# A four-layer hybrid trunk: another order of the attention layer's sums, and a last down projection over the 512 output positions

## The reference

```python
def mla_mixer(a, w_down, g_cq, g_ckv, w_uq, w_ukv, g_qhead, g_khead, w_o, cos, sin, cid):
    down = a @ w_down
    c_q = rms_norm(down[..., :384], g_cq);  c_kv = rms_norm(down[..., 384:640], g_ckv);  k_pe = down[..., 640:]
    q = (c_q @ w_uq).reshape(B, L, 8, 192);  kv = (c_kv @ w_ukv).reshape(B, L, 8, 256)
    k = concatenate([kv[..., :128], k_pe for every head]);  v = kv[..., 128:]
    q = rms_norm(q, g_qhead);  k = rms_norm(k, g_khead)          # then rope on the last 64
    # real queries in blocks of 128 see the keys of their own and earlier chunks of 64 and the meta tokens
    s = q k^T * 192 ** -0.5;  p = softmax(mask(s));  o = p v
    return o @ w_o

def conv_glu_ffn(a, w_up, conv_w, conv_b, w_down):
    u = causal_depthwise_conv3(a @ w_up, conv_w) + conv_b
    gate, val = split(u, 2)
    return (silu(gate) * val) @ w_down

def reference(...):
    h = concatenate([meta_tokens (16), x (512)])                 # 528 positions, D = 1024
    for layer in range(4):
        h = h + mixer[layer](rms_norm(h));  h = h + conv_glu_ffn(rms_norm(h))
    return h[:, 16:]
```

## Time and profile before

| what | value |
|---|---|
| median of three runs | 3211.4 us (3210.82 to 3211.84) |
| profiled execution | 3212.88 us |
| its span, first to last instruction | 3211.1 us |
| mean granted TensorE clock | 0.948 of 2.4 GHz |
| attention layer, about | 30 to 400 us |
| last down projection, about | 3078 to 3211 us |

### The profile page before, as it was taken

The page is one execution under the profiler, slowest core; times in us unless marked ns, Lnnn a source line. Parts: engine busy times, 40 slices in busy tenths (PEclk is TensorE's granted clock), DMA queues, the critical chain, the costliest instruction groups (busy, mean ns, idle before and its releaser), DMA issues.

```text
span 3211.1 us, 59360 instructions
## 1 busy us (share of the span) xinstructions
PE 2908.4 (91%) x23040; PEld 2763.9 (86%) x23040; DVE 2089.1 (65%) x2751; ACT 972.1 (30%) x1411; POOL 1409.3 (44%) x667
## 2 busy tenths in 40 slices
PE   6687899999888879998965799999999999899999
PEld 5566799999888879998964799999999898799999
DVE  4677568871466667888979658883335435678840
ACT  2122233432333323333235333333212122222221
POOL 4211155565322225555453255556534243355563
PEclk9698899999999989999987899999999999999999
DMA  3011022233211112222220022223322232122232
GB/s 119 27 34 31 27 80 87 87 96 106 77 52 52 52 34 79 85 86 84 88 74 1 27 86 81 85 89 105 116 88 72 73 93 73 40 72 86 87 109 79
DMA packets 66413, 234.52 MB, mean 73 GB/s; under 512 B 8145, under 2 KB 8913, under 8 KB 65777
## 3 DMA queue, kind: packets, MB, share of 16 engines
q1 hardware_dynamic: 63648, 225.70, 23.2%
q10 hardware_dynamic: 2640, 7.02, 0.7%
HBM read 230.60 MB, written 2.10 MB: 72 GB/s over the span
## 4 chain that ended last, share of the span: by engine, by line
PE 49%; DVE 31%; issue 13%; ACT 2%; DVEq 2%; POOL 2%; DMA 0%; ACTq 0%; POOLq 0%
PE ps L224 37%; DVE scr L432 8%; DVE scr L429 6%; DVE ub L423 4%; DVE scr L426 3%; PE ps L246 2%; PE ps L1878 1%; PE ps L1372 1%; ACT work L1673 1%; DVEq L426 1%; DVE work L1052 1%; DVE work L799 1%; PE ps L997 1%; PE ps L237 1%; PE ps L1357 1%
## 5 line engine op out<-in xcount | busy, mean ns | idle before, releaser
L224 PE MATMUL ps<-xs,wr 128*128 128x264 f32 x13056 | 1659.6, 289 | 70.1 <-POOL xs L342 30.4
L224 PEld LDWEIGHTS ps<-xs,wr 128*128 128x128 f32 x13056 | 1623.7, 192 | 101.7 <-issue 61.8
L212 POOL TENSOR_TENSOR wr<-raw,wr 128x1024 fp32r<-128x1024 f32 x422 | 1101.9, 2615 | 1221.9 <-ACT wr L204 1219.4
L224 PE MATMUL ps<-hid,wr 128*128 128x264 f32 x6528 | 803.9, 286 | 23.6 <-POOL wr L212 17.0
L224 PEld LDWEIGHTS ps<-hid,wr 128*128 128x128 f32 x6528 | 799.4, 190 | 26.9 <-POOL wr L212 19.0
L204 ACT ACTIVATE wr<-raw 128x1024 fp32r<-128x1024 f32 x422 | 441.2, 1050 | 403.2 <-PE ps L224 399.5
L432 DVE SCALAR_TENSOR_TENSOR scr<-ub,convp,scr 128x528 f32<-128x528 f32 x176 | 469.2, 2666 | 24.0 <-DVE scr L429 0.6
L500 POOL TENSOR_TENSOR hid<-scr,hid 128x528 f32 x88 | 136.3, 1549 | 223.7 <-ACT hid L472 223.7
L429 DVE SCALAR_TENSOR_TENSOR scr<-ub,convp,scr 128x528 f32<-128x528 f32 x176 | 205.1, 1166 | 26.6 <-DVE scr L426 17.4
L448 DVE TENSOR_TENSOR h<-ps,h 128x528 f32 (+1 forms) x32 | 22.6, 707 | 291.3 <-PE ps L224 291.1
L472 ACT ACTIVATE hid<-scr 128x528 f32 x88 | 56.9, 646 | 405.4 <-DVE scr L438 405.4
(11 more groups left out here) (251 smaller groups left out, 2330.7 us busy)
## 6 DMA issues: line engine op xcount, KB each, us to landing
raw<-in_stream SPq DMA_DIRECT2D x422, 512.0 KB, 3.6
work<-in_ret_tab ACTq DMA_DIRECT2D x4, 1056.0 KB, 5.6
h<-in_h SPq DMA_DIRECT2D x8, 264.0 KB, 6.6
out<-h SPq DMA_DIRECT2D x8, 256.0 KB, 4.6
work<-in_s_b ACTq DMA_DIRECT2D x1, 512.0 KB, 3.6
work<-in_s_c ACTq DMA_DIRECT2D x1, 512.0 KB, 4.6
convp<-in_convp ACTq DMA_DIRECT2D x4, 88.0 KB, 2.0
work<-in_mla_tab ACTq DMA_DIRECT2D x1, 264.0 KB, 2.6
```

The costliest lines, as they stand in the source:

```text
L212: pool.tensor_tensor(wr[:, s, 1].rearrange("p a b -> p (a b)"), raw[:, s, :], wr[:, s, 0].rearrange("p a b -> p (a b)").bitcast(F32), ALU. ...
L224: mm = pe.matmul(out[:, q], wr[:, slot, w, b0 + k], x[k][v][:, q * HALF:(q + 1) * HALF], start=start and k == 0 and p == 0, stop=stop and ...
```

## The change

It has two parts.

The attention order. The sums leave the tile of the transposed v. In `X_SEQ` they come right behind the fifth scores ("S", 4) and share that entry's tile (`tile_of`): the scores lie in its columns 0 to 15, the sums from column 640 on. The fifth scores' reciprocal then counts on a semaphore step of its own ("shared") instead of releasing the tile, and the means of the sums release it. The value projection moves behind ("O", 1), and the transposes of v with their two copies become an entry "vt" with a tile of its own behind the spreads. So an `X_SEQ` walk still takes 22 tiles. In `P_SEQ` "sum" comes ahead of "vv", with a tile of its own, and "vt" is the eighth tile. The instructions are the same in number and size.

The last down projection. In the last feed-forward part alone, `project_real` multiplies the 512 real positions in one matmul, in one bank, where `project` had two of 264. VectorE adds 512 columns to `h` instead of 528.

```diff
+        def project_real(pe, out, slot, x, start, stop, inc, before):
+
+            for k in range(len(x)):
+                if k in before:
+                    pe.wait_ge(*before[k])
+                for p, (w, v) in enumerate(((0, 0), (0, 1), (1, 0))):
+                    mm = pe.matmul(out[:, 0:SEQ], wr[:, slot, w, k], x[k][v][:, META:T],
+                                   start=start and k == 0 and p == 0, stop=stop and k == len(x) - 1 and p == 2)
+            mm.then_inc(inc, 1)
...
+                        if last:
+                            project_real(pe, flat(gg + m), u % RING, x, j == 0, j == 2, unit_done, before)
+                        else:
+                            project(pe, tile(gg + m), u % RING, 0, x, j == 0, j == 2, unit_done, before)
...
+                if last:
+                    hm = h[:, m + 4 * i, META:T]
+                    dve.tensor_tensor(hm, flat(gg + m)[:, 0:SEQ], hm, ALU.add).then_inc(tile_free, 1)
+                else:
+                    hm = h[:, m + 4 * i].rearrange("p (a b) -> p a b", a=2)
+                    dve.tensor_tensor(hm, tile(gg + m), hm, ALU.add).then_inc(tile_free, 1)
...
-            P_SEQ = ["qn", "qr", "kn", "vv", "sum", "spreadq", "spreadk"]
+            P_SEQ = ["qn", "qr", "kn", "sum", "vv", "spreadq", "spreadk", "vt"]
...
-            X_SEQ = [("S", 0), ("S", 1), "qn", ("T", 0), ("S", 2), "qr", ("O", 0), "kn", ("T", 1), ("S", 3),
-                     "vv", ("T", 2), ("S", 4), ("O", 1), "sum", ("T", 3), ("O", 2), ("T", 4), "spreadq",
-                     "spreadk", ("O", 3), ("O", 4)]
+            X_SEQ = [("S", 0), ("S", 1), "qn", ("T", 0), ("S", 2), "qr", ("O", 0), "kn", ("T", 1), ("S", 3), ("T", 2),
+                     ("S", 4), "sum", ("O", 1), "vv", ("T", 3), ("O", 2), ("T", 4), "spreadq", "spreadk", "vt",
+                     ("O", 3), ("O", 4)]
+
+            def tile_of(seq, k):
+
+                return k - (seq is X_SEQ and k >= seq.index("sum"))
+            X_TILES = len(X_SEQ) - 1
...
-            p_dve = Order(sem("mla_p_dve"), ["up", "down", "turned", "vt", "vtm"] +
+            p_dve = Order(sem("mla_p_dve"), ["up", "down", "turned", "shared"] +
                           [("f", s) for s in ["mean0"] + NEWTON + ["root"]] +
-                          ["qr", "kn", "kr"])
+                          ["qr", "kn", "kr", "vt"])
             p_act = Order(sem("mla_p_act"), ["sqqn", "sqqr", "sqkn"])
-            p_pe = Order(sem("mla_p_pe"), ["qn", "kn", "sum", "spreadq", "spreadk"])
+            p_pe = Order(sem("mla_p_pe"), ["qn", "kn", "sum", "spreadq", "spreadk", "vt"])
...
+            W2 = 2 * X_TILES
+            assert W2 % 4 == 0
...
+                    if s != "sum" or g < gX:
+                        pe.wait_ge(tile_free, g - 3 + i * W2)
...
-                    elif s == "sum":
-
-
+                    elif s == "vt":
                         pe.wait_ge(tile_free, vv_at(g) + 1 + i * W2)
                         for b in range(QB):
                             pe.transpose(flat(g)[:, b * P:(b + 1) * P], vfm[:, META + b * P:META + (b + 1) * P], ident[:])
-                        pe.transpose(flat(g)[0:META, 512:512 + P], vfm[:, 0:META], ident[:])
+                        pe.transpose(flat(g)[0:META, 512:512 + P], vfm[:, 0:META], ident[:])\
+                            .then_inc(p_pe.sem, p_pe.one("vt"))
+                    elif s == "sum":
+
                         pe.wait_ge(p_act.sem, p_act.done("sqkn", h0) + i * 2 * len(p_act.names))
                         sums_pe(pe, g, SUM_Q, [(sqn, P), (sqr, ROPE)])
                         sums_pe(pe, g, SUM_K, [(sqk, P), (sqkr, ROPE)]).then_inc(p_pe.sem, p_pe.one("sum"))
...
-                        pe.wait_ge(p_dve.sem, p_dve.done("vtm", h0) + i * 2 * len(p_dve.names))
+                        pe.wait_ge(p_dve.sem, p_dve.done("vt", h0) + i * 2 * len(p_dve.names))
...
+                    elif s == "vt":
+                        dve.wait_ge(p_pe.sem, p_pe.done("vt", h0) + i * 2 * len(p_pe.names))
+                        dve.tensor_copy(vt[j][:, 0:512], flat(g)[:, 0:512]).then_inc(p_dve.sem, p_dve.one("vt"))
+                        dve.tensor_copy(vt[j][0:META, 512:512 + P], flat(g)[0:META, 512:512 + P]).then_inc(tile_free, 1)
                     elif s == "sum":
+                        if g < gX:
+                            dve.sem_inc(p_dve.sem, p_dve.one("shared"))
                         dve.wait_ge(p_pe.sem, p_pe.done("sum", h0) + i * 2 * len(p_pe.names))
-                        dve.tensor_copy(vt[j][:, 0:512], flat(g)[:, 0:512]).then_inc(p_dve.sem, p_dve.one("vt"))
-                        dve.tensor_copy(vt[j][0:META, 512:512 + P], flat(g)[0:META, 512:512 + P])\
-                           .then_inc(p_dve.sem, p_dve.one("vtm"))
                         mean_rsqrt(dve, g, [SUM_Q, SUM_K], QK, roots, scratch, p_dve, "f", h0 + 2 * i,
...
-                        dve.reciprocal(st[:, 3:4], st[:, 2:3]).then_inc(tile_free, 1)
-                        dve.wait_ge(tile_free, g + 1 + i * W2)
+                        inverse = dve.reciprocal(st[:, 3:4], st[:, 2:3])
+                        if b == QB and g < gX + X_TILES * (HEADS - 1):
+                            inverse.then_inc(p_dve.sem, p_dve.one("shared"))
+                            dve.wait_ge(p_dve.sem, p_dve.done("shared", h0 + 1) + i * 2 * len(p_dve.names))
+                        else:
+                            inverse.then_inc(tile_free, 1)
+                            dve.wait_ge(tile_free, g + 1 + i * W2)
...
-                    ffn_pe(pe, n, int(name[3]) - layer0, u0, g0)
+                    ffn_pe(pe, n, int(name[3]) - layer0, u0, g0, n == len(at) - 1 and not DEBUG)
```

More of the change, by code:

```diff
@@ L376, in setup_of, with ffn_pe @@
             return mixer[n].get("setup") if n in mixer else None
-        def ffn_pe(pe, n, layer, u0, g0):
+        def ffn_pe(pe, n, layer, u0, g0, last):
             x = split_tiles(xs, range(DT))
@@ L406, in ffn_pe @@
                         pe.wait_ge(lo_ready, u + 1 + i * 12)
-                        project(pe, tile(gg + m), u % RING, 0, split_tiles(hid, range(k0, k0 + nb)),
-                                j == 0, j == 2, unit_done, {k - k0: w for k, w in late.items()})
+                        x, before = split_tiles(hid, range(k0, k0 + nb)), {k - k0: w for k, w in late.items()}
+                        if last:
+                            project_real(pe, flat(gg + m), u % RING, x, j == 0, j == 2, unit_done, before)
+                        else:
+                            project(pe, tile(gg + m), u % RING, 0, x, j == 0, j == 2, unit_done, before)
                         k0 += nb
@@ L446, in down @@
                 dve.wait_ge(unit_done, ug + 3 * m + 3 + i * 12)
-                hm = h[:, m + 4 * i].rearrange("p (a b) -> p a b", a=2)
-                dve.tensor_tensor(hm, tile(gg + m), hm, ALU.add).then_inc(tile_free, 1)
-                if not last:
+                if last:
[4 more added lines that the diff above has]
+                    dve.tensor_tensor(hm, tile(gg + m), hm, ALU.add).then_inc(tile_free, 1)
                     dve.wait_ge(tile_free, gg + m + 1 + i * 4)
@@ L551, in mla @@
             uO = uH + 2 * HEADS
[L552 removed]
+            gO = gX + X_TILES * (HEADS - 1) + len(A_SEQ)
             assert gO + DT == g0 + 1 + MLA_TILES
```

23 lines of the change are left out of this document (11 added, 12 removed).

## The result

The changed kernel takes 3184.2 us in the median (3183.9 to 3185.0, 4 runs) against 3211.5 beside it (3210.8 to 3211.8, 4 runs): a ratio of 0.9916, 95% interval [0.9902, 0.9931]. It is 27.3 us faster; the forecast was 3191 (20.4 faster), its range 3178 to 3203. The profiled execution took 3184.01 us, with a span of 3182.2. Against the span of before the 28.9 us went as follows; masks are the first mask of a head (line 770 before, 799 after), and the output projection of attention begins at 380.90 before and 353.18 after.

A forecast was written before the change was run, and what follows sets the result against it. Bound: one serial VectorE-TensorE-VectorE loop per attention head, and TensorE alone in the last down projection. Terms 3.7 + 5.4 + 10.3 + 1 = 20.4 us, giving 3191 us, range 3178 to 3203.

The forecast's parts named there:

- rival (c): Attention: fewer pauses, head 0 and half the heads' spreads at 2.4 GHz; 9 us more gain, 3182 us; chance 0.17.
- Last down projection: Last feed-forward stage, bound by TensorE alone: wide matmuls save 0.53 us in each of 7 tiles, 3.7 us (0 to 11.6).
- by column: Last down projection: matmul excess grows with columns; 234 ns at 512 columns (233 taken), 15.4 us a tile.
- a fixed cost per matmul: Last down projection, rival (a): 10.6 ns per matmul is fixed, 224 ns each; 7.9 us instead of 3.7, 3187; chance 0.22.
- The reason given for it: Last down projection: a lone 264-column fp32r matmul lasts 173 ns over its streaming, 7 more than fp32; excess partly inside the matmul.
- Prologue: P_SEQ: sums run before the value projection, so VectorE starts the means at 101.43 instead of 106.83; 5.4 us.
- Heads: X_SEQ, seven heads: 1.47 us each from the new order, 10.3 us, plus 1 us for the value projection's clock.
- The replay's own part: Head with means at 214.24 replayed: no wait for sums, spread 0.9 us behind the chain, mask at 225.2 instead of 226.70.
- the assumption that the spreads stay at 1.2 GHz: Heads: spreads keep the 0.50 clock, 3.7 us, VectorE waiting about 1.8 us; 2.4 GHz would save up to 1.4 more.
- 1 us in three heads: Heads: value projection slowed by low clock in some heads would lie under the Newton chain; 1 us (0 to 1.7).
- rival (d): Attention: shifted pauses leave the clock at 0.50 through every head's scores, 4.4 us a head; slower, 3227; chance 0.04.
- nothing later than the layer can absorb the gain: Attention layer: every layer waits for the one before, so a microsecond off VectorE's chain is one off the span.

The follow-up runs named there:

- three others of the new order: Profiles of the attention order alone run again (3190.2 us), the changed kernel with one more VectorE instruction (3193.4) and with eight more (3181.0).
- the two profiles of the changed kernel: The changed kernel's first profiled run (3184.01 us) and that of its unaltered rerun (3200.62 us; the rerun's median is 3185.6).
- eight instructions more: Eight VectorE instructions that only wait for what has long come, added to the changed kernel ahead of the first feed-forward layer; 3181.0 us, ratio 0.9908.
- the projection alone: Only the wide matmuls of the last down projection and the 512-column addition put into the kernel before, attention order kept; 3206.5 us, ratio 0.9987.
- the one profile without a low clock in the attention layer: First profile (3172.16 us) of the changed kernel with idle matmuls in and ahead of the attention layer and eight more waiting VectorE instructions.
- The kernel with the lowest median of this study: The changed kernel plus idle identity matmuls in TensorE's pauses in and ahead of the attention layer, and eight waiting VectorE instructions; 3177.0 us, again 3177.8.

## Why the prediction was right, and where not

The bound was read rightly: one serial loop per head, in which VectorE's time is the span's. The time fell inside the range and nearest to rival (c); the forecast was 6.8 us too high. That it came so near is in part luck. By the spans of the two profiles (by the medians it is 27.3) the kernel gained 28.9 us where 20.4 was forecast, and the 8.5 between are a balance: 7.8 more in the heads, 1.6 in the prologue, 1.0 in the last projection, 1.6 ahead of the layer and 2.3 in stretches that had no term, less the 5.8 that the feed-forward loops lost.

**Last down projection**: 0.66 us a tile instead of 0.53, 4.65 in all instead of 3.7. The choice (by column, not a fixed cost per matmul) held: 231.0 ns, where by column alone gave 234 and the fixed cost 224. From 264 and 512 columns follow 0.445 ns a column and 3.0 ns a matmul. The reason given for it was only half right: the lone matmul lasts 387 ns, 174 over its streaming, as at 264 columns (173), so the lone one does not slow down by column; only the stream of them does. The first tile gained nothing, as said.

**Prologue**: 5.4 forecast, 7.0 measured up to the mask. The chain moved by 6.1 after the start's 1.6: the 5.4 of the forecast to the tenth, and 0.7 ahead of it, where VectorE waited 1.45 us for the second projection (line 759) instead of 2.16. The other 0.9 lie between the spread and the mask, where the clock rose for 3.4 us.

**Heads**: 10.3 + 1 forecast, 16.3 measured, and 2.8 more behind head 7's mask. The split is that of one profile: in three others of the new order the steps take 219.6 us and the last head 22.5 to 22.6, and the sum is the same within 0.6 us. The replay's own part came true line by line: no wait for the sums, the spread 0.9 behind the chain (234.90 + 0.43 to 236.28: 0.95), no wait at the mask. The step that failed is the assumption that the spreads stay at 1.2 GHz, with a wait of 1.8 before them: the value projection under the chain fills the pause that brought the low clock, and the wait became 0.87 or less in five of the seven steps. In the replayed step's terms: from the spread's start to the mask the prediction had 7.2 us (218.0 to 225.2), measured are 5.98, while ahead of the spread it had 1.6 less than before and 1.8 was measured. Rival (c) had this mechanism, with a chance of 0.17, and priced it at 1.4 us a spread, near the 1.0 to 1.7 that lie behind the spread's start when the value projection is moved back. It looked for the cause in fewer pauses, not in this projection. The prediction listed the value projection as a step that costs nothing and gains 1 us in three heads; that it is TensorE's filler was in none of its sentences.

**Clock**: the prediction took the pauses of one profile as a property of the kernel. They are one of several patterns: the same kernel's steps took 31.0 in one run and 34.4 in another, and rival (d)'s place for the low clock, given 0.04, occurs in three steps of each of the two profiles of the changed kernel. What (d) had wrong is the number of heads and so the sign.

**Feed-forward loops**: + 5.8 us (5.0 net of what the next stretch gives back), in no step and no rival. The sentence that nothing later than the layer can absorb the gain was right for the order of the work and still missed that four instructions earlier in the list change the pace of loops later in it. With eight instructions more the same change measures 3181.0.

## What to carry to other kernels

Where TensorE waits for a serial chain on another engine, put its least urgent matmuls there: here they cost nothing, and in five of seven steps what stands behind the chain ran at full clock. Filling one of several pauses only moved the low clock, and with all of one layer's filled, other layers had more of it; compare more than one profile before a price is put on it. And when stages change that the edit does not touch, compare the pace of their loops and the gap before each instruction: a list that has become a few instructions longer can cost, or give back, as much as the edit itself.

## What the runs showed of the hardware

- Single places in VectorE's list of instructions cost 0.10 us each time a loop passes them; by tipping the meeting with GpSimd it cost 0.39 us a pair of tiles, 4.2 us in the second layer's loop. Four instructions that only wait made the kernel before 4.9 us slower (ratio 1.0017 [1.0008, 1.0026]).
- A stream of fp32r matmuls with a fresh weight load each takes 120.6 ns at 264 columns and 231.0 at 512 (230.0 in the profile of the projection alone), at a granted clock of 1.00; a lone one 173 to 174 ns over its streaming at either width.
- In the one profile without a low clock in the attention layer six of seven steps take 31.0 us and the seventh 30.4. The kernel with the lowest median of this study (3177.0 and 3177.8, ratios 0.9921 and 0.9909) still has runs of 3200, which are unexplained; by the ratio it is no faster than the changed kernel with the eight instructions alone (0.9908 [0.9894, 0.9922]).
